# Row norms and loads reordered at the front, transposes ahead of values, and the last norms shared by three engines

## The chip, the cores and the metric
One core of a Trainium2 chip runs the whole program. The metric is the device time of one execution in microseconds (us), the median over runs.

## What is computed
One decoder block over 1024 tokens of width 1024, in float32, from `x`, 256 memory tokens `mem` and the weights. Cut to what matters:

```python
h = rms_norm(x, g_in);  proj = h @ w_in        # q,k,v of groups A,B,M, gate, index q,k,w
kvM = rms_norm(mem, g_mem) @ w_mem_kv
oA = dilated_mixture_attention(qA, kA, vA)     # 8 heads, three windows
oB = dsa_attention(qB, kB, vB, qI, kI, wI)     # 4 heads, top 256 keys by index score
oM = memory_attention(qM, kM, vM)              # 4 heads, 256 memory keys
o = concat(oA, oB, oM) * silu(gate)
return rms_norm(x + o @ w_out, g_final)
```

## The kernel before
The program is written by hand: each engine has its own instruction list, and semaphores join them. SyncE (SP) issues every DMA. Tokens are worked on in 8 tiles ("rows") of 128. Every large product is made three times, from a high and a low part of each operand (high x high, high x low, low x high), so each operand needs a high part (a copy on ScalarE, ACT) and a low part (a difference, on VectorE, DVE, or GpSimd, POOL).

**Front.** SP loads rows 0 to 3, weight tile 0, rows 4 to 7, the two memory rows, weight tile 1, two memory weights and, after a wait, weight tile 2 (L521 to L533). All weight tiles go through one buffer, `w_raw`; `load_w` (L504) waits until both parts of the tile before are made. `split_hi` (L736) makes the high part on ACT, `split_lo` (L643) the low part on POOL. The norm of a row is a sum of squares (`square_sum`: ACT L722 or DVE L992), a variance (DVE L971), a root (ACT L734), four small linked DVE instructions (L976 to L979) and a scaling of the row (DVE L1012); `scale_rows` does this for rows 0 and 1, 2 and 3, 4 to 7, and the memory rows. TensorE (PE) transposes the rows of a half (`turn`, L1307) into six PSUM banks; ACT makes the high part of each of the eight transposed blocks (`high`, L799), DVE the low part (`low`, L981). A bank comes free with its low part. `fill` (L1330) is a projection of one weight tile for one half of the tokens: fills 0 and 2 are tile 0 (halves 0 and 1), fills 1 and 3 tile 1. `evacuate` (L744) takes a fill out of PSUM, on ACT, and `split_low` (L1026) makes its low part, on DVE. `turn_mem` and `keep_mem` (L806) transpose the memory rows. The first index score needs the evacuation of w_i, which stands on ACT behind evacuation 3, the split of tile 3 and the eight `keep_mem`.

**Steps.** 8 pairs of heads (M, A, A, A, A, B, B, M) of 8 query tiles each are 64 steps; step 64 only finishes. On PE (loop at L1569) a step is: `scores` of step s, `turn_prob` (L1461) of the first four key tiles of step s-1, half of a fill, `values` (L1475) of these key tiles, then, if step s-1 had more than four key tiles, `turn_prob`, the other half of the fill and `values` for the rest. Not every step has a fill: those of pair 4 at tiles 4 and 5, pair 5 at 0 and 1, pair 6 at 2, 4, 6 and 7, and all of pair 7 have none. `values` waits for both copies of the transposed probabilities, head a by ACT (L899) and head b by DVE (L1198). DVE's step (loop at L1252) is: bias of head a (L1189 or L1176), copy, bias of head b, slots of the top-256 selection in pairs 0 to 5 (L1110 to L1144), second copy, the end of a group of four tiles (L1216, L1220), `split_low`. ACT's step is: copy, exponent of head a, second copy, exponent of head b, splits of weights, evacuation. In pair 6 the output weights are split too (ACT L939, low parts on POOL L706 and DVE L1289).

**End.** From step 56 on PE also does the output projection (`project_out`, L1527, 24 matmuls a unit), whose units DVE adds to the residual rows `y_rows` (`add_out`, L1222). In step 63 DVE norms rows 0 and 1 (`norm_rows`, L1246: variance, root on ACT, four links, final product L1243) and SP stores them. In step 64 come the last copy of probabilities and values, `turn_sums` (L1512), the end of the last group, POOL's `part_lo` (L668) and the last unit (3, 1). Then `project_last` (L1555) adds pair 7's part to rows 4 to 7, `add_last` (L1229) adds them, and rows 2 to 5 and 6 to 7 are normed in two chains. ACT squares each row (`square_row`, L877).

What orders the end on DVE and ACT are these lines:

```python
for n in range(len(LATE)):          # DVE L1297
    add_last(n)
norm_rows(1, 2, 6)
norm_rows(2, 6, 8)
```

## Time and profile before

| what | us |
|---|---|
| median of 3 runs | 780.11 (778.83 to 781.57) |
| profiled execution, its own time | 775.92 |
| span in the profile | 774.1 |
| busy: PE / DVE / ACT / POOL | 692.8 / 440.6 / 331.6 / 132.6 |
| mean granted TensorE clock | 0.969 |

The span runs from the first to the last instruction of one execution. Busy time is that of an engine's instructions without waits; matmuls overlap, so a busy PE is not PE at its peak. The granted clock is 1 at 2.4 GHz and 0.5 at 1.2 GHz.

### The profile page before, as it was taken

The page shows a single profiled execution, that of the slowest core. Times are in us where ns is not written, and L with a number is a line of the kernel's source. Part 1 is how long each engine was busy: PE and PEld are TensorE (multiplying, and loading weights), DVE is VectorE, ACT ScalarE, POOL GpSimd, SP SyncE. Part 2 cuts the span into 40 slices and gives each one's busy share as a digit, 9 for nine tenths or more (in the row PEclk, how much of TensorE's full clock was granted, in tenths as well). Part 3 has the DMA queues.
Part 4 walks back from the last instruction along what each step waited for, and adds up shares of the span by engine and source line. Part 5 has one row for each costly group of instructions (what it writes and reads, how often), then busy time and mean ns, then how long its engine had stood idle before and what let it go on. Part 6 is the DMA issues. An engine that isn't in the chain of part 4 may idle for free.

```text
span 774.1 us, 11520 instructions
## 1 busy us (share of the span) xinstructions
PE 692.8 (89%) x4261; PEld 546.9 (71%) x4261; DVE 440.6 (57%) x1003; ACT 331.6 (43%) x627; POOL 132.6 (17%) x90
## 2 busy tenths in 40 slices
PE   2879999999999999999999996979899868999972
PEld 2667788777777777777777774757677656777761
DVE  4856775265377448655876587679743354122237
ACT  4666565335335433543354353435444554121313
POOL 1121110111131122113111311031132124102000
PEclk9999999999999999999999997999999998999997
DMA  8311112111211022102212111010114206310014
GB/s 303 94 55 27 28 29 81 28 28 41 83 54 55 3 83 69 41 14 82 56 42 67 44 40 42 1 41 1 41 28 150 83 21 235 97 37 21 0 55 163
DMA packets 51863, 47.71 MB, mean 62 GB/s; under 512 B 5712, under 2 KB 44640, under 8 KB 51808
## 3 DMA queue, kind: packets, MB, share of 16 engines
q1 hardware_dynamic: 51808, 46.97, 19.4%
q8 instruction: 35, 0.57, 0.3%
q14 instruction: 20, 0.16, 0.1%
HBM read 39.62 MB, written 7.34 MB: 61 GB/s over the span
## 4 chain that ended last, share of the span: by engine, by line
PE 75%; DVE 12%; issue 5%; ACT 4%; DMA 1%; POOL 1%; DVEq 0%; SPq 0%; ACTq 0%; POOLq 0%
PE j_ps L1365 23%; PE s_ps L1365 8%; PE o_ps L1496 8%; PE pt_ps L1472 7%; PE s_ps L1401 5%; PE s_ps L1547 4%; PE j_ps L1547 4%; DVE picked L1114 4%; PE o_ps L1365 3%; PE s_ps L1420 3%; PE pt_ps L1420 2%; DVE probT L1198 1%; DVE prob L1189 1%; PE pt_ps L1518 1%; PE s_ps L1552 1%
## 5 line engine op out<-in xcount | busy, mean ns | idle before, releaser
L1365 PE MATMUL j_ps<-h_hi,w_hl 128*128 128x512 f32 (+2 forms) x640 | 210.4, 394 | 0.9 <-issue 0.9
L1365 PEld LDWEIGHTS j_ps<-h_hi,w_hl 128*128 128x128 f32 (+1 forms) x640 | 120.1, 189 | 25.5 <-issue 1.5
L647 POOL TENSOR_TENSOR w_hl<-w_raw,w_hl 128x1024 fp32r<-128x1024 f32 (+1 forms) x30 | 70.9, 2365 | 341.5 <-ACT w_hl L742 341.5
L1365 PE MATMUL j_ps<-h_lo,w_hl 128*128 128x512 f32 (+2 forms) x320 | 123.4, 386 | 0.0
L911 ACT ACTIVATE prob<-prob,nmax 128x256 f32<-128x256 f32 (+7 forms) x128 | 89.9, 703 | 50.9 <-DVE nmax L1189 47.3
L899 ACT ACTIVATE probT<-pt_ps 128x512 f32<-128x512 f32 (+3 forms) x88 | 41.4, 471 | 162.3 <-PE pt_ps L1472 161.8
L1472 PE MATMUL pt_ps<-ident,prob 128*128 128x128 f32 x496 | 75.8, 289 | 7.7 <-DVE gate L1216 7.3
L1365 PE MATMUL s_ps<-h_hi,w_hl 128*128 128x512 f32 x224 | 73.8, 398 | 0.4 <-POOL w_hl L647 0.4
L1472 PEld LDWEIGHTS pt_ps<-ident,prob 128*128 128x128 f32 x496 | 55.0, 144 | 24.8 <-issue 21.6
L1114 DVE TENSOR_SCALAR_CACHE_REDUCE picked<-idx,tk 128x384 f32<-128x384 f32 (+5 forms) x72 | 67.9, 943 | 1.6
L1365 PEld LDWEIGHTS j_ps<-h_lo,w_hl 128*128 128x128 f32 (+1 forms) x320 | 60.6, 189 | 11.1
L1198 DVE COPY probT<-pt_ps 128x512 f32<-128x512 f32 (+3 forms) x88 | 46.7, 531 | 27.5 <-PE pt_ps L1472 26.8
L1189 DVE CUSTOM_DVE_ANT_0 prob<-s_ps,bias 128x128 f32<-128x128 f32 (+7 forms) x64 | 47.1, 753 | 24.1 <-PE s_ps L1401 20.8
L1042 DVE SCALAR_TENSOR_TENSOR qk<-j_ps,qk 128x512 fp32r<-128x512 f32 (+2 forms) x28 | 17.7, 633 | 61.9 <-ACT qk L778 39.1
L1091 DVE SCALAR_TENSOR_TENSOR idx<-prob,w_i,idx 128x384 f32<-128x384 f32 (+5 forms) x42 | 40.2, 972 | 20.9 <-ACT prob L849 20.7
L1496 PE MATMUL o_ps<-probT,v_sb 128*64 128x128 f32 x576 | 42.8, 284 | 8.9 <-DVE probT L1198 7.8
L1496 PEld LDWEIGHTS o_ps<-probT,v_sb 128*64 128x64 f32 x576 | 31.1, 138 | 25.1 <-issue 22.7
L1365 PEld LDWEIGHTS s_ps<-h_hi,w_hl 128*128 128x128 f32 x224 | 42.1, 188 | 9.2 <-issue 0.6
L1365 PE MATMUL s_ps<-h_lo,w_hl 128*128 128x512 f32 x112 | 43.6, 390 | 0.0
L1496 PE MATMUL o_ps<-probT,v_b 128*64 128x128 f32 x288 | 22.6, 294 | 17.8 <-DVE probT L1198 17.8
L1401 PE MATMUL s_ps<-qk 64*128 64x512 f32 (+3 forms) x288 | 36.5, 376 | 0.0
L1365 PE MATMUL o_ps<-h_hi,w_hl 128*128 128x512 f32 (+1 forms) x96 | 33.8, 392 | 2.8 <-POOL w_hl L647 2.8
(233 smaller groups left out, 1091.7 us busy)
## 6 DMA issues: line engine op xcount, KB each, us to landing
w_raw<-in_w_in_dram SPq DMA_DIRECT2D x28, 512.0 KB, 3.9
idx<-in_x_dram SPq DMA_DIRECT2D x8, 512.0 KB, 5.9
bias<-in_a_tab_dram SPq DMA_DIRECT2D x8, 512.0 KB, 5.1
mixed_scratch<-gate SPq DMA_DIRECT2D x12, 256.0 KB, 2.2
bias<-in_x_dram SPq DMA_DIRECT2D x4, 512.0 KB, 8.3
probT<-in_w_mem_kv_dram SPq DMA_DIRECT2D x4, 512.0 KB, 6.3
bias<-in_w_out_dram SPq DMA_DIRECT2D x4, 512.0 KB, 3.8
out_dram<-idx SPq DMA_DIRECT2D x4, 512.0 KB, 2.8
```

The lines of the kernel that those rows point to most:

```text
L647: pool.tensor_tensor(w_hl[:, w % 2, 1, :, 0:n], w_raw[:, :, 0:n], w_hl[:, w % 2, 0, :, 0:n].bitcast(F32), ALU.subtract).then_inc(w_lo_read ...
L899: act.activation(probT[:, g % 2, 0, 0:n, :], pt_ps[0][:, 0:n, :], ACT.Copy).then_inc(pt_ready[0], 1)
L911: act.activation(prob[:, a, s % 2, 0:n], prob[:, a, s % 2, 0:n], ACT.Exp, scale=-1.0, bias=nmax[:, a, s % 2:s % 2 + 1], accum_out=lsum[:, ...
L1091: dve.scalar_tensor_tensor(out=x_slice(i), in0=relu[u % 4][:, 0:n], scalar=wt, in1=x_slice(i), op0=ALU.mult, op1=ALU.add).then_inc(idx_add ...
L1114: link(dve.tensor_scalar(some, xs, level, None, ALU.is_ge, ALU.add, accum_out=count))
L1189: dve.tensor_tensor_reduce(dst, s_ps[a][:, 0:n], table, scale, 3e38, ALU.add, ALU.min, low_out).then_inc(biased[a], 1)
L1198: dve.tensor_copy(probT[:, g % 2, 1, 0:n, :], pt_ps[1][:, 0:n, :]).then_inc(pt_ready[1], 1)
L1365: last = pe.matmul(bank[0:n, at:], a[:, k, 0:n], c[:, k, HALF * b + at:HALF * b + HALF], start=(k == 0 and q == 0), stop=(k == KD - 1 and ...
L1401: last[a] = pe.matmul(banks[a][:, keys], q[rows, tile], k[rows, keys], start=(m == 0), stop=(m == 2))
L1472: last = pe.transpose(pt_ps[a][:, n, :], prob[:, a, s % 2, P * k:P * k + P], ident[:, :])
L1496: last = pe.matmul(o_ps[DH * a:DH * a + DH, at], v, probT[:, g % 2, a, n, :], start=(k == 0), stop=(k == nk - 1))
L1547: pe.matmul(bank, a[:, p, :], wo_half(c, p, b), start=(p == 0 and q == 0), stop=False)
```

## The change
Three parts, in one diff.

1. Front: weight tile 1 gets a buffer of its own (`gate`, not yet in use) and is loaded right after tile 0, ahead of rows 4 to 7; tile 2 no longer waits for tile 1. Rows 0 to 3 share one norm chain. ACT scales the last row of each chain of four (rows 3 and 7), DVE the others. On ACT the split of tile 1 and the squares of rows 4 and 6 move ahead of the first eight high parts, the memory rows' root and evacuation 3 move forward. On DVE the square of row 5 moves ahead of the low parts. POOL waits for four scaled rows before its first split.
2. Steps: on PE the first `values` move behind the second `turn_prob` and the second half of the fill. This changes the order only where step s-1 had more than four key tiles.
3. End: rows 0, 1 and 2 are normed in step 64, behind the last copies of probabilities, with ACT's squares in step 63. Rows 3 to 7 share one chain; POOL multiplies rows 3 and 4 by the gain, ACT scales them, DVE does rows 5 to 7 as before.

```diff
-FINAL_ORDER = [0, 1, 2, 3, 4, 5, 6, 7]
+EARLY_ROWS = [0, 1, 2]
+SHARED_ROWS = [3, 4]
+LAST_ROWS = [5, 6, 7]
...
+        w_raws = [w_raw[:, :, :], gate[:, :].rearrange("p (k m) -> p k m", k=KD)]
...
+        def raw_of(w):
+            return w_raws[w == 1]
...
         def _(sp):
             def load_w(w):
-                if w:
-                    sp.wait_ge(w_hi_ready, w)
-                    sp.wait_ge(w_lo_ready, w)
+                if w >= 2:
+                    before = w if w > 2 else 1
+                    sp.wait_ge(w_hi_ready, before)
+                    sp.wait_ge(w_lo_ready, before)
                 at = 0
                 for c, n in W_TILES[w][2]:
-                    sp.dma_start(w_raw[:, :, at:at + n], w_k[:, :, c:c + n]).then_inc(w_in_sem, 16)
+                    sp.dma_start(raw_of(w)[:, :, at:at + n], w_k[:, :, c:c + n]) \
+                        .then_inc(w_second_in if w == 1 else w_in_sem, 16)
...
             load_w(0)
+            load_w(1)
             for r in range(NT // 2, NT + MT):
                 load_rows(r)
-            load_w(1)
+            load_w(2)
             load_wm(0)
             load_wm(1)
-            load_w(2)
...
-            for n, t in enumerate(FINAL_ORDER):
+            for n, t in enumerate(EARLY_ROWS):
                 sp.wait_ge(y_final, n + 1)
+                sp.dma_start(out_t[t], y_rows[t]).then_inc(stored, 16)
+            for n, t in enumerate(SHARED_ROWS):
+                sp.wait_ge(y_scaled, n + 1)
+                sp.dma_start(out_t[t], y_rows[t]).then_inc(stored, 16)
+            for n, t in enumerate(LAST_ROWS):
+                sp.wait_ge(y_final, len(EARLY_ROWS) + n + 1)
                 sp.dma_start(out_t[t], y_rows[t]).then_inc(stored, 16)
...
+            pool.wait_ge(x_ready, NT // 2)
             for w in range(PRE_W + 1):
                 split_lo(w)
...
             part_lo(STEPS)
+            for t in SHARED_ROWS:
+                pool.wait_ge(ysq_ready, t + 1)
+                pool.tensor_tensor(y_rows[t], y_rows[t], gf_row, ALU.mult).then_inc(y_gained, 1)
...
+            def scale_row(r, chain):
+                act.wait_ge(x_inverse, chain)
+                act.activation(x_raw[r], x_raw[r], ACT.Copy, scale=stat[:, 3, r:r + 1]).then_inc(x_ready, 1)
+
             square_sum(0)
             square_sum(2)
-            root(0, 2)
             square_sum(3)
+            root(0, 4)
             split_hi(0)
-            root(2, 4)
+            scale_row(3, 1)
+            split_hi(1)
+            square_sum(4)
+            square_sum(6)
             act.wait_ge(g_ready, 1)
             for v in range(KD):
                 high(v)
-            square_sum(4)
-            square_sum(6)
-            split_hi(1)
             root(4, 8)
             evacuate(0)
+            scale_row(7, 2)
             for v in range(KD, 2 * KD):
                 high(v)
             evacuate(1)
             square_sum(NT)
             square_sum(NT + 1)
+            root(NT, NT + MT)
             evacuate(2)
             split_hi(2)
-            root(NT, NT + MT)
+            evacuate(3)
             for k in range(KD):
                 keep_mem(k)
-            evacuate(3)
             split_hi(3)
...
+                if s == STEPS:
+                    y_root(0, 0, len(EARLY_ROWS))
                 if s in PART_AT:
                     part_hi(s)
                 if s == STEPS - 1:
-                    square_row(0)
-                    square_row(1)
-                    y_root(0, 0, 2)
+                    for t in EARLY_ROWS:
+                        square_row(t)
...
-            square_row(2)
-            for t in range(3, NT):
+            for t in range(len(EARLY_ROWS), NT):
                 square_row(t)
-                if t in (5, 7):
-                    y_root(1 + t // 7, 2 if t == 5 else 6, t + 1)
+            y_root(1, len(EARLY_ROWS), NT)
+            act.wait_ge(y_inverse, 1)
+            for n, t in enumerate(SHARED_ROWS):
+                act.wait_ge(y_gained, n + 1)
+                act.activation(y_rows[t], y_rows[t], ACT.Copy, scale=stat[:, 3, t:t + 1]).then_inc(y_scaled, 1)
...
                 inverse_root(a, b)
-                for r in range(a, b):
+                dve.drain().then_inc(x_inverse, 1)
+                for r in range(a, b if a >= NT else b - 1):
                     dve.tensor_scalar(x_raw[r], x_raw[r], stat[:, 3, r:r + 1], None, ALU.mult).then_inc(x_ready, 1)
...
-            scale_rows(0, 2, 1)
-            scale_rows(2, 4, 3)
+            scale_rows(0, 4, 3)
+            square_sum(5)
             for v in range(KD):
                 low(v)
-            square_sum(5)
             square_sum(7)
             scale_rows(4, 8, 5)
...
                 if early[1]:
                     add_out(*early[1])
+                if s == STEPS:
+                    start_norm(0, 0, len(EARLY_ROWS))
                 if s >= 1 and (s - 1) % 4 == 3:
                     finish_group(pair_of_step(s - 1)[0], (s - 1) % NT // 4)
+                if s == STEPS:
+                    dve.wait_ge(gf_in, 16)
+                    for t in EARLY_ROWS:
+                        final_norm(t)
                 if early[2]:
                     add_out(*early[2])
-                if s == STEPS - 1:
-                    norm_rows(0, 0, 2)
...
                 add_last(n)
-            norm_rows(1, 2, 6)
-            norm_rows(2, 6, 8)
+            start_norm(1, len(EARLY_ROWS), NT)
+            dve.drain().then_inc(y_inverse, 1)
+            for t in LAST_ROWS:
+                final_norm(t)
...
                     project_out(*early[0])
-                if s >= 1:
-                    values(s - 1, 0)
                 if two:
                     turn_prob(s - 1, 1)
-                if early[1]:
-                    project_out(*early[1])
                 if s < STEPS and projection_of_step(s):
                     if two:
                         fill(m, range(KD // 2, KD))
                     m += 1
+                if early[1]:
+                    project_out(*early[1])
+                if s >= 1:
+                    values(s - 1, 0)
                 if two:
                     values(s - 1, 1)
```

## Rows read from the trace of the kernel before

**Rows 1.** the page: busy time of the engines, and POOL's costliest group
```profile
PE 692.8 (89%) x4261; PEld 546.9 (71%) x4261; DVE 440.6 (57%) x1003; ACT 331.6 (43%) x627; POOL 132.6 (17%) x90
...
L647 POOL TENSOR_TENSOR w_hl<-w_raw,w_hl 128x1024 fp32r<-128x1024 f32 (+1 forms) x30 | 70.9, 2365 | 341.5 <-ACT w_hl L742 341.5
```

**Rows 2.** waits of PE: releaser, us in total, times, longest
```profile
PE o_ps L1496 <- DVE probT L1198: 29.9, 16, 4.4
```

**Rows 3.** timeline of the front: start us, us, engine, line, operation [idle before]
```profile
9.55 1.06 ACT L727 ACTIVATE prob<-idx 128x1024 f32<-128x1024 f32 x1 [0.17 <-DMA idx<-in_x_dram]
...
9.82 0.91 SPq L514 DMA_DIRECT2D bias<-in_x_dram  x2
...
12.17 0.99 DVE L977 SCALAR_TENSOR_TENSOR stat<-stat 128x2 f32<-128x2 f32 x1
...
13.59 1.42 DVE L1012 TENSOR_SCALAR idx<-idx,stat 128x1024 f32<-128x1024 f32 x2
...
16.28 1.48 ACT L803 ACTIVATE h_hi<-s_ps,g_cols 128x512 fp32r<-128x512 f32 x2 [4.34 <-PE s_ps L1314]
...
29.24 0.38 PE L1365 MATMUL o_ps<-h_hi,w_hl 128*128 128x256 f32 x1 [2.83 <-POOL w_hl L647]
...
33.71 0.27 PE L1314 MATMUL s_ps<-ident,picked 128*128 128x128 f32 x1
...
35.07 1.41 DVE L986 SCALAR_TENSOR_TENSOR h_lo<-s_ps,g_cols,h_hi 128x512 fp32r<-128x512 f32 x2 [0.56 <-ACT h_hi L803]
```

**Rows 4.** DMA issues of the first 30 us: count, size, us to landing
```profile
bias<-in_x_dram SPq DMA_DIRECT2D x2, 512.0 KB, 6.0
```

**Rows 5.** busy time by stretch: 10 to 19 us, with clock, DMA share, GB/s
```profile
10.00:19.00 9.00, 3.93 (x19) 3.94 (x20) 6.41 (x13) 3.87 (x8) 1.40 (x1) 1.00 1.01 369
```

**Rows 6.** timeline around the first index score
```profile
46.21 2.17 DVE L977 SCALAR_TENSOR_TENSOR stat<-stat 128x2 f32<-128x2 f32 x1
...
56.15 0.22 ACT L756 ACTIVATE w_i<-pt_ps 128x64 f32<-128x64 f32 x1
...
56.62 0.70 PE L1420 MATMUL s_ps<-kk_b,qk 128*128 128x384 f32 x2 [2.17 <-DVE qk L1042]
```

**Rows 7.** timeline, start of pair 5
```profile
502.78 1.39 DVE L1042 SCALAR_TENSOR_TENSOR qk<-j_ps,qk 64x512 fp32r<-64x512 f32 x2 [2.65 <-ACT qk L782]
...
506.43 3.26 POOL L694 TENSOR_SCALAR idx<-picked 128x896 f32<-128x896 f32 x1 [17.38 <-DVEq L1159]
...
512.47 1.76 DVE L1110 TENSOR_SCALAR rungs<-rungs,reach 128x13 f32<-128x13 f32 x1
```

**Rows 8.** timeline, end of pair 6
```profile
626.98 1.09 PE L1496 MATMUL o_ps<-probT,v_b 128*64 128x128 f32 x16 [1.78 <-DVE probT L1198]
...
629.26 0.66 PE L1496 MATMUL o_ps<-probT,v_b 128*64 128x128 f32 x8 [0.61 <-DVE probT L1198]
...
631.80 2.55 DVE L1289 SCALAR_TENSOR_TENSOR h_lo<-bias,h_hi 128x1024 fp32r<-128x1024 f32 x1 [2.69 <-ACT h_hi L939]
...
639.55 1.55 PE L1496 MATMUL o_ps<-probT,v_b 128*64 128x128 f32 x12 [0.74 <-DVE probT L1198]
...
648.73 1.09 PE L1496 MATMUL o_ps<-probT,v_b 128*64 128x128 f32 x16 [0.88 <-DVE probT L1198]
```

**Rows 9.** timeline of the end
```profile
746.03 0.77 PE L1496 MATMUL o_ps<-probT,v_m 128*64 128x128 f32 x8 [4.39 <-DVE probT L1198]
...
760.08 1.23 DVE L1234 TENSOR_TENSOR idx<-s_ps,idx 128x1024 f32<-128x1024 f32 x1 [0.16 <-PE s_ps L1566]
...
768.47 2.48 DVE L1243 SCALAR_TENSOR_TENSOR idx<-idx,stat,w_raw 128x1024 f32<-128x1024 f32 x2
```

**Rows 10.** DMA issues of the last 34 us: the stores of rows 4 to 7
```profile
out_dram<-idx SPq DMA_DIRECT2D x4, 512.0 KB, 2.8
```

**Rows 11.** busy time by stretch: the end, and one us of stores
```profile
742.00:764.00 22.00, 14.01 (x60) 10.84 (x60) 13.27 (x24) 7.99 (x16) 1.30 (x1) 0.91 0.12 49
...
771.00:772.00 1.00, 0.00 (x0) 0.00 (x0) 0.00 (x0) 0.00 (x0) 0.00 (x0) 0.50 1.00 401
```

More of the change, by code:

```diff
@@ L369, in build_program @@
         w_in_sem = sem("w_in_sem")
+        w_second_in = sem("w_second_in")
+        x_inverse = sem("x_inverse")
         w_hi_ready = sem("w_hi_ready")
@@ L417, in build_program @@
         y_final = sem("y_final")
+        y_gained = sem("y_gained")
+        y_inverse = sem("y_inverse")
+        y_scaled = sem("y_scaled")
         stored = sem("stored")
@@ L646, in split_lo @@
                 n = width(w)
-                pool.tensor_tensor(w_hl[:, w % 2, 1, :, 0:n], w_raw[:, :, 0:n],
+                pool.tensor_tensor(w_hl[:, w % 2, 1, :, 0:n], raw_of(w)[:, :, 0:n],
                                    w_hl[:, w % 2, 0, :, 0:n].bitcast(F32), ALU.subtract).then_inc(w_lo_ready, 1)
@@ L736, in split_hi @@
             def split_hi(w):
-                act.wait_ge(w_in_sem, 16 * sum(len(W_TILES[q][2]) for q in range(w + 1)))
+                if w == 1:
+                    act.wait_ge(w_second_in, 16)
+                else:
+                    act.wait_ge(w_in_sem, 16 * sum(len(W_TILES[q][2]) for q in range(w + 1) if q != 1))
                 if w >= 2:
@@ L741, in split_hi @@
                 n = width(w)
-                act.activation(w_hl[:, w % 2, 0, :, 0:n], w_raw[:, :, 0:n], ACT.Copy).then_inc(w_hi_ready, 1)
+                act.activation(w_hl[:, w % 2, 0, :, 0:n], raw_of(w)[:, :, 0:n], ACT.Copy).then_inc(w_hi_ready, 1)
             def evacuate(m):
@@ L1244, in final_norm @@
                                          op0=ALU.mult, op1=ALU.mult).then_inc(y_final, 1)
-            def norm_rows(n, a, b):
-                dve.wait_ge(gf_in, 16)
-                start_norm(n, a, b)
-                for t in range(a, b):
-                    final_norm(t)
             for s in range(STEPS + 1):
```

## The prediction

> **What bounds the kernel now.** I read the busy shares first: TensorE (PE) is busy for 692.8 of 774.1 us [rows 1], so time can only come out of its remaining 81 us. The waits of PE come second: its largest releaser is VectorE's (DVE's) copy of the transposed probabilities, 29.9 us in 16 waits, the longest 4.4 [rows 2]. The timelines then show where the idle time lies: a front up to the first index score at 56.62 [rows 3, 6], the steps of pairs 4 to 6 [rows 7, 8], and the end from 742 on [rows 9, 11]. Between these, in pairs 1 to 3 and from 650 to 742, matmuls follow one another, and a move of work between other engines is worth nothing there. The change touches all three places with idle time.
>
> **The front.** (a) One norm chain for rows 0 to 3 takes the place of two. The third square of ScalarE (ACT) starts at 9.55 and takes 1.06 plus 0.2 for its sum [rows 3]. Before, the second chain had a link of 0.99 us where its like take 0.16 [rows 3]: it ran into the first split product of GpSimd (POOL), which the new wait on four scaled rows keeps away. One chain is about 1.3 us, to 12.1; DVE scales three rows at 0.71 each (1.42 for two to 15.0 [rows 3]), ACT the fourth in 1.06 beside it: ready at 14.2, before at 15.0. Gain 0.8.
>
> (b) This gain is lost at once. The squares of rows 4 and 6 now stand ahead of the first half's eight high parts on ACT. Row 6 was issued at 9.82 [rows 3] and landed about 6.0 us later (median of rows 6 and 7) [rows 4], so near 15.5. The second weight tile, 512 KB at 369 GB/s [rows 5], comes in ahead of it and costs 1.4 to 1.8 us: row 6 is there at 17.1. The square ends at 18.35; the first high part, before at 16.28 [rows 3], starts 2.1 us late. On DVE the square of row 5 reads two SBUF operands, and POOL's two split products (1.4 us for the 72-column tile and 2.4 [rows 1]) run from 14.2 to 18.0. DVE operations of that kind are seen held to the end of a POOL product: 0.99 and 2.17 for 0.16 [rows 3, 6], 2.55 for 1.23 [rows 8]. I take the hold; the low parts then start at 19.7, not 17.0. The Trainium skill, SBUF — State Buffer, "Who interferes with whom", has the same pair as an exclusive lock for the whole instruction, won by whoever starts first. By that rule DVE could also win and hold POOL, and the sum would be 0.6 better.
>
> (c) What pays is the wait behind it. PE used to stand 2.83 us for the second tile's low part, and its next 24 matmuls took from 29.24 to 33.7 [rows 3], 0.19 us each, with a clock that had fallen in the wait. That tile is now split by 18.0. With eight low parts at 0.7 each (1.41 for two [rows 3]) from 19.7, the first fill ends at 26.9 (before 26.4), and the second follows without a wait, 24 matmuls at the full clock (0.12 each, an estimate), to 29.8. Rows 4 to 7: DVE is free of low parts at 25.3, square 1.65, chain 1.2, three scalings 2.1: 30.2, against a first transpose at 33.71 [rows 3]. Gain 3.5.
>
> (d) The memory rows' chain now stands ahead of ACT's evacuation and split. Its link of 2.17 under a POOL product [rows 6] goes, and with it PE's 1.9 us before their transposes. Evacuation 3 moves ahead of the eight keeps. The last thing before the first score stays ACT's evacuation of w_i: it ended at 56.37, the score started at 56.62 [rows 6]. New: fill 3 ends at 48.3 - 3.5 = 44.8, evacuation 1.2, eight keeps 3.0, split 1.06, w_i 0.2, which is 50.5, and the score at 50.8. **Front: -5.8.** Ends: -3.0 if the second tile costs twice as much of the load queue, -6.6 with no hold.
> The new wait of POOL has nothing behind it but these splits. SyncE's new place for tile 2 makes the memory weights wait until about 16, and nobody needs them before 100.
>
> **Transposes ahead of values.** No instruction is added. In steps with a fill the second values cost nothing either way. What changes there is that the fill ends one group of values (1.1 us) earlier, so that its evacuation and split do. In pairs 0 to 3 PE is without gaps, so nothing follows. In pair 4 the step without a fill waits for a DVE that is busy with the selection; a copy behind those slots is not earlier. Nothing.
> Pair 5: DVE idles 2.65 us for the evacuated query at 502.78 [rows 7]. With the fill 1.1 us earlier its split, bias and copy come 0.7 earlier (then the transposes bind), and so does POOL's mask at 506.43. The selection starts when POOL's split ends, at 514.2 (the 1.76 us row at 512.47) [rows 7], and PE follows this chain to 544. **-0.7**, ends 0 and -0.9. That PE's own wait before the second values at 508 shortens is worth nothing, since POOL's end starts the selection.
> Pair 6, steps 53 to 56, three of them without a fill. The waits before the second values, 0.61, 0.74 and 0.88 [rows 8], vanish, since the first values now cover the copy: 2.2. Beyond that, the earlier transposes release ACT's second exponent and then its output-weight splits by 0.9 us, and the DVE split that runs 2.55 us under a POOL product [rows 8] ends earlier by as much; the first wait (1.78 [rows 8]) shrinks by 0.7 by the earlier fill. Followed through to the end of the step at 650 I get 1.3 more. **-3.5**, ends -2.2 (the three waits alone) and -4.1.
>
> **The end.** Before, DVE normed rows 0 and 1 ahead of the last copy of probabilities, and PE stood 4.39 us until 746.03 [rows 9]. Now the copy goes first: values at about 742.5, -3.5. PE's clock was below full in this stretch, 0.91 over 22 us [rows 11], which is 2 us of work; most of that follows the stall, and I count 1.5. Against it: three final products of 1.24 [rows 9] stand ahead of the addition that opens rows 3 to 7, with POOL's 1.3 us product between them, which costs 0.5. So the last addition, at 760.08 [rows 9], comes at 755.6 and ends at 756.8. Square 1.25 to 758.1, chain 1.2 to 759.3.
> From there three last rows on DVE take 3.7 us, to 763.0, where before the last two began at 768.47 and ended at 770.95 [rows 9]. ACT scales rows 3 and 4 by 760.4 and 761.5, with POOL's two gain products (2.4 each, from 752.6) done by 757.5. But five stores now come together: one takes 2.7 to 2.8 us [rows 10] and each further one 1.3 (512 KB at 401 GB/s [rows 11]): 760.45 + 2.7 + 4 x 1.3 = 768.4. So the stores are late next, not DVE (763.0 + 2.8 = 765.8). The span ended at 774.1, 0.4 after the last landing: **-5.4**, ends -3.5 (the stall goes, and nothing else) and -6.7.
>
> **Sum.** 5.8 + 0.7 + 3.5 + 5.4 = 15.4 us. The profiled execution took 775.92, with a span of 774.1: 760.5 and a span near 758.7. It is 4.2 below the median of the runs, so the forecast for the median is 780.11 - 15.4 = 764.7. The ends add up to 8.7 and 18.3, or 771.4 and 761.8.
>
> **Rivals.** (1) DVE and ACT still set the pace in pairs 5 and 6 and the new order gives nothing: 15.4 - 4.2 = 11.2, 768.9. For it: the copies wait behind bias and weight splits on DVE. Against: three waits come after a DVE that idled. Chance 0.14. (2) The front is held by loads: row 6 lands at 20 instead of 17.1 because the strided weight tile goes through slowly, and ACT's high parts stand behind its square. Front -2.9, 767.6. For it: the queue is full throughout. Chance 0.13. (3) The end gives only its stall, 3.5 instead of 5.4, because POOL's products come late or hold DVE's chain: 766.6. Chance 0.12. (4) Slower: the same place as (2), one us of the whole for each us that row 6 is late. To eat 15.4 us it would have to land after 32, and nothing in the profile is that slow. That the whole lands within 0.3% would want 30. Chance 0.02, with 0.02 more for no change. The forecast as worked out has 0.57.
>
> 0.3% (2.3 us) is about what a measurement of this kernel can tell from no change. Faster by more 0.95, same 0.03, slower 0.02. The range reaches over (1) to (3) and over two of them together, and takes in the spread of the runs: 760.5 to 771.5.
>
> **What would show it.** First transpose near 14.2 and first high part near 18.3; no wait before the second fill; first index score near 50.8. The mask of pair 5 0.7 us closer to its step's start, and no waits before second values in pair 6. PE's wait of 4.4 us at the end below 1, the last final product near 763 and five stores back to back. The forecast is wrong if ACT waits for row 6 well past 17, if the score stays later than 53, or if the waits named as the probabilities' copies keep their 29.9 us.

## The result, and the profile after

The changed kernel takes 752.66 us, median of 4 runs (752.36 to 755.78); the kernel before, run beside it, 779.47 (4 runs, 778.33 to 781.57). The ratio is 0.9662, 95% interval [0.9628, 0.9696]: 26.8 us faster, where 15.4 were forecast. The forecast median was 764.7, and 760.5 was the low end of the range. The profiled execution of after took 752.36, with a span of 750.6. One run each of before, before_again and order_without_fill took between 1003 and 2340 us; the ratios leave these three slow runs out.

The page of after, its busy times; the span's 774.1 became 750.6 and PE's idle time went from 81 to 66 us:

```profile
PE 684.3 (91%) x4261; PEld 546.1 (73%) x4261; DVE 437.9 (58%) x989; ACT 335.5 (45%) x629; POOL 137.3 (18%) x92
```

PE's busy time fell too, by 8.5 us [rows 1], with the same 4261 matmuls. That is the first sign that idle time is not all that was saved: in the experiments below it changes with the granted clock and with the order of the same matmuls.

The waits of PE after (releaser, us in total, times, longest), which answer to [rows 2]:

```profile
PE o_ps L1532 <- DVE probT L1234: 13.1, 9, 3.7
PE s_ps L1350 <- DVE idx L1049: 11.8, 1, 11.8
PE pt_ps L1508 <- DVE gate L1252: 7.2, 9, 2.9
PE pt_ps L1508 <- DVE probT L1234: 5.5, 4, 3.0
```

The 29.9 us before the values are 13.1, and 5.5 of what went is back as a wait of the second transposes: their PSUM bank is free only when DVE has copied the first ones.

To compare kernels whose times shift, I read in each trace when PE starts the first index score, step 0, and the transposes of the sums that close each half of a pair, and took differences. Time of each stage in us, two profiles of each kernel (the second ones are the unchanged kernels run again, below); stages of a pair run from the close of the pair before to its own:

```
stage                        before  again    after  again   mean gain   forecast
start to first index score    56.62  57.91    51.00  52.03      5.8        5.8
index scores to step 0        89.75  86.66    86.61  88.21      0.8        0
step 0 to close of pair 3    291.44 290.79   287.73 287.47      3.5        0
pairs 4 and 5                147.34 147.62   146.23 144.93      1.9        0.7
pair 6                        64.59  67.75    60.53  59.76      6.0        3.5
pair 7 and the end           124.35 124.80   118.46 118.47      6.1        5.4
span                         774.10 775.54   750.57 750.87     24.1       15.4
```

**The front.** Timeline of after (columns as in [rows 3]):

```profile
12.65 2.08 DVE L1049 TENSOR_SCALAR idx<-idx,stat 128x1024 f32<-128x1024 f32 x3
14.79 3.42 PE L1350 MATMUL s_ps<-ident,idx 128*128 128x128 f32 x16 [11.75 <-DVE idx L1049]
...
16.18 2.36 POOL L668 TENSOR_TENSOR w_hl<-gate,w_hl 128x1024 fp32r<-128x1024 f32 x1
16.27 2.82 DVE L1031 CUSTOM_DVE_ANT_0 prob<-dist 128x512 f32<-128x512 f32 x1 [1.54 <-DMA dist<-in_x_dram]
17.54 1.06 ACT L752 ACTIVATE prob<-bias 128x1024 f32<-128x1024 f32 x1 [1.41 <-DMA bias<-in_x_dram]
...
18.59 2.41 ACT L831 ACTIVATE h_hi<-s_ps,g_cols 128x512 fp32r<-128x512 f32 x4
...
19.13 0.69 DVE L1033 CUSTOM_DVE_ANT_0 prob<-dist 128x512 f32<-128x512 f32 x1
...
20.06 2.73 DVE L1022 SCALAR_TENSOR_TENSOR h_lo<-s_ps,g_cols,h_hi 128x512 fp32r<-128x512 f32 x4
```

ACT's high parts wait for the square of row 6, which waits 1.41 us for its load. DVE's square of row 5 takes 2.82 us where its second half takes 0.69: it starts 0.09 us after POOL's product and ends at 19.09, 0.55 us after that one. Then the second fill follows the first without a wait, where [rows 3] had 2.83 us:

```profile
27.16 0.40 PE L1401 MATMUL j_ps<-h_hi,w_hl 128*72 128x512 f32 x1
...
27.39 0.28 PE L1401 MATMUL o_ps<-h_hi,w_hl 128*128 128x256 f32 x1
...
30.68 0.33 PE L1350 MATMUL s_ps<-ident,picked 128*128 128x128 f32 x1 [0.27 <-ACT bias L845]
...
51.00 0.59 PE L1456 MATMUL s_ps<-kk_b,qk 128*128 128x384 f32 x2 [1.64 <-ACT w_i L784]
```

**The end.** Timeline of after, which answers to [rows 9]:

```profile
724.76 0.66 PE L1532 MATMUL o_ps<-probT,v_m 128*64 128x128 f32 x8 [0.77 <-DVE probT L1234]
...
737.43 1.23 DVE L1270 TENSOR_TENSOR idx<-s_ps,idx 128x1024 f32<-128x1024 f32 x1
738.69 1.06 ACT L918 ACTIVATE qk<-idx 128x1024 fp32r<-128x1024 f32 x1 [0.21 <-DVE idx L1270]
...
741.25 3.67 DVE L1279 SCALAR_TENSOR_TENSOR idx<-idx,stat,w_raw 128x1024 f32<-128x1024 f32 x3 [0.16 <-DVE stat L1015]
...
742.36 0.33 SPq L650 DMA_DIRECT2D out_dram<-bias  x1
743.40 0.33 SPq L650 DMA_DIRECT2D out_dram<-idx  x1
743.78 2.74 SPq L653 DMA_DIRECT2D out_dram<-idx  x3
```

PE's wait of 4.39 is 0.77. DVE is done at 744.9, but the five stores, issued from 742.36 to 745.33, land at 745.02, 746.29, 747.59, 748.94 and 750.16, one every 1.3 us, and the span ends 0.4 later. In between the queue is full (busy time of one us; DMA share and GB/s are the last columns):

```profile
748.00:749.00 1.00, 0.00 (x0) 0.00 (x0) 0.00 (x0) 0.00 (x0) 0.00 (x0) 0.50 1.00 401
```

### The profile page after: what moved, and what is told of

Same layout as the page of the kernel before. It is cut to its first block, busy times and chain, and to the rows that moved or that the text cites. A ratio compares the mean times of both kernels' runs of the same rounds, so it can differ in the third digit from the quotient of the medians.

```text
span 750.6 us, 11512 instructions
## 1 busy us (share of the span) xinstructions
PE 684.3 (91%) x4261; PEld 546.1 (73%) x4261; DVE 437.9 (58%) x989; ACT 335.5 (45%) x629; POOL 137.3 (18%) x92
## 4 chain that ended last, share of the span: by engine, by line
PE 74%; DVE 12%; issue 5%; ACT 4%; POOL 2%; DMA 1%; SPq 1%; DVEq 0%; ACTq 0%; POOLq 0%
PE j_ps L1401 24%; PE s_ps L1401 8%; PE pt_ps L1508 7%; PE o_ps L1532 7%; PE s_ps L1437 5%; PE s_ps L1583 5%; PE j_ps L1583 4%; DVE picked L1150 4%; PE o_ps L1401 4%; PE s_ps L1456 3%; PE pt_ps L1456 2%; DVE prob L1225 1%; PE s_ps L1588 1%; DVE tk L1153 1%; PE pt_ps L1554 1%
## 5 line engine op out<-in xcount | busy, mean ns | idle before, releaser
L668 POOL TENSOR_TENSOR w_hl<-w_raw,w_hl 128x1024 fp32r<-128x1024 f32 (+1 forms) x29 | 68.2, 2353 | 327.3 <-ACT w_hl L770 314.8
L1401 PE MATMUL s_ps<-h_hi,w_hl 128*128 128x512 f32 x224 | 74.7, 402 | 0.3 <-POOL w_hl L668 0.3
L1225 DVE CUSTOM_DVE_ANT_0 prob<-s_ps,bias 128x128 f32<-128x128 f32 (+7 forms) x64 | 47.0, 753 | 26.8 <-PE s_ps L1437 23.9
L1234 DVE COPY probT<-pt_ps 128x512 f32<-128x512 f32 (+3 forms) x88 | 46.7, 531 | 14.8 <-PE pt_ps L1508 13.7
L1532 PE MATMUL o_ps<-probT,v_sb 128*64 128x128 f32 x576 | 40.1, 283 | 4.5 <-DVE probT L1234 4.5
L1401 PE MATMUL s_ps<-h_lo,w_hl 128*128 128x512 f32 x112 | 44.1, 394 | 0.0
L1583 PE MATMUL s_ps<-h_hi,w_hl 128*128 128x512 f32 x96 | 31.9, 400 | 0.0
```

Of the source, the lines that this page charges most:

```text
L668: pool.tensor_tensor(w_hl[:, w % 2, 1, :, 0:n], raw_of(w)[:, :, 0:n], w_hl[:, w % 2, 0, :, 0:n].bitcast(F32), ALU.subtract).then_inc(w_lo_ ...
L1225: dve.tensor_tensor_reduce(dst, s_ps[a][:, 0:n], table, scale, 3e38, ALU.add, ALU.min, low_out).then_inc(biased[a], 1)
L1234: dve.tensor_copy(probT[:, g % 2, 1, 0:n, :], pt_ps[1][:, 0:n, :]).then_inc(pt_ready[1], 1)
L1401: last = pe.matmul(bank[0:n, at:], a[:, k, 0:n], c[:, k, HALF * b + at:HALF * b + HALF], start=(k == 0 and q == 0), stop=(k == KD - 1 and ...
L1532: last = pe.matmul(o_ps[DH * a:DH * a + DH, at], v, probT[:, g % 2, a, n, :], start=(k == 0), stop=(k == nk - 1))
L1583: pe.matmul(bank, a[:, p, :], wo_half(c, p, b), start=(p == 0 and q == 0), stop=False)
```

## The experiments

Each kernel is timed against the kernel before, in runs on the same chip; the interval is the 95% one. A ratio can differ by up to 0.002 from the quotient of the medians. The question was where the 9 us by which the spans fell beyond the forecast (24.1 for 15.4) come from.

### The three parts alone, and the kernel before once more

Each is one part of the diff and nothing else: the row chains and loads (front_only), the order on PE (order_only), the last rows (end_only). before_again is the unchanged kernel.

> Only the order on PE is changed (values behind the second transposes and the second half of the fill); front and end are those of before. Theory: PE pays for each change between values and other matmuls, about 0.3 us in each of the 12 wide steps with a fill of pairs 1 to 3, so pairs 1 to 3 shorten by 3.7 us, pairs 4 and 5 by about 1.1 and pair 6 by about 4: -8.8 us, a span near 765.3. Rival (the prediction): steps with a fill are worth nothing, -4.2 us, a span near 769.9, and pairs 1 to 3 as long as before.

> Only the front of the change (loads, row chains, squares, memory chain). Theory: the first index score comes at 51.0 instead of 56.6 (-5.6), and pairs 1 to 3 stay as long as before. If the two falls of the clock in the index scores (from 56.9 and 77.4) stay away as in the changed kernel, 3.2 us more: -8.8 in all, a span near 765.3. Rival: the falls belong to the single execution and not to the change, then -5.6, a span near 768.5.

> Only the end of the change (rows 0 to 2 normed in step 64, one chain for rows 3 to 7, three engines). Theory: -5.9 us, of which PE's wait for the last copy of probabilities gives 3.6 and the fall of the clock behind it 1 to 1.5; everything up to 741 as before, a span near 768.2. Rival: the gain at the end needs the earlier parts (loads or clock), then -3.5.

> The kernel before, unchanged, with a profile of its own. Theory: the clock falls in the index scores come and go from one execution to the next, so this profile may lack one or both and be up to 3.4 us shorter up to 140 us; the profiled executions are no sure sign of the median. Rival: the falls come after the same waits every time, then the first 140 us agree with the first profile within 0.3 us. Ratio to before 1.000.

```
kernel        median  ratio    interval            span
order_only    766.78  0.9848   [0.9824, 0.9873]    764.8
front_only    773.83  0.9934   [0.9911, 0.9958]    770.6
end_only      771.45  0.9924   [0.9899, 0.9948]    769.7
before_again  778.54  1.0014   [0.9989, 1.0039]    775.5
```

The front alone gives 5.1 us (0.66% of 778.5) and the end 5.9: both near their terms, 5.8 and 5.4. The order alone gives 11.8, where its terms were 0.7 and 3.5. Multiplied, the three ratios make 0.9709, inside the interval of the second measurement of the whole (0.9703, below). So the error sits in the order on PE. order_only gives more than the 8.8 us that were expected of it, 11.8 in the medians and 9.3 in the spans.

before_again shows what a single profile is worth. Between the first index score and step 0 the kernel does the same in all of these (busy time of that stretch; after its length come PE, PEld, DVE, ACT, POOL, the granted clock, DMA share, GB/s). The kernel before:

```profile
56.60:146.40 89.80, 84.25 (x410) 72.06 (x410) 52.40 (x64) 48.00 (x71) 9.11 (x4) 0.96 0.13 36
```

before_again:

```profile
57.90:144.60 86.70, 81.16 (x410) 69.37 (x410) 52.36 (x64) 47.99 (x71) 9.11 (x4) 1.00 0.14 37
```

after:

```profile
51.00:137.60 86.60, 81.08 (x408) 69.31 (x409) 52.44 (x64) 47.99 (x71) 9.23 (x4) 1.00 0.14 37
```

order_only:

```profile
55.80:147.00 91.20, 85.69 (x408) 73.35 (x408) 52.00 (x64) 47.94 (x71) 9.05 (x4) 0.95 0.13 35
```

The idle time (length less PE) is 5.5 us in all four. What differs is PE's busy time, and with it the clock. In the traces the granted clock falls from 1 to 0.5 (1.2 GHz) for a short while. There are two such falls in the first row (at 56.95 and 77.43), none in the second and third, three in the fourth (55.58, 76.06 and 96.54). Each is worth about 1.5 us: 3.2 and 4.6 us of busy time above the rows that have none.

They are of two kinds. The later ones stand behind two waits of 1.8 us inside the stretch, which are the same in every kernel here. Behind these two, 5 of the 16 profiles of this document have no fall, 7 have one and 4 have two, with the old front (5 falls in 7 profiles) and with the new (10 in 9). Nothing ties those to the change. The first one belongs to the front: each of the seven profiles with the old front has a fall that starts between 51.1 and 57.0, behind the memory rows' chain and the wait for w_i, in some before the first index score and in some behind it. Of the nine with the new front only memory_old_place (below), which puts that chain back, has one there, at 48.34. So of the 3.1 us by which after beats the first profile of before in this stretch, half is that fall and half is chance.

### Which steps gain from the order

Two kernels have the new order in one kind of step each: in steps with a fill, or in those without (`late = not (...)`).

```diff
-                if s >= 1:
+                late = bool(s < STEPS and projection_of_step(s))
+                if s >= 1 and not late:
                     values(s - 1, 0)
                 if two:
                     turn_prob(s - 1, 1)
-                if early[1]:
-                    project_out(*early[1])
...
+                if early[1]:
+                    project_out(*early[1])
+                if s >= 1 and late:
+                    values(s - 1, 0)
```

A third, values_between, puts the first values between the second transposes and the second half of the fill. The transposes come early, as in the change, but PE still goes to the values twice.

```diff
-                if s >= 1:
-                    values(s - 1, 0)
                 if two:
                     turn_prob(s - 1, 1)
-                if early[1]:
-                    project_out(*early[1])
+                if s >= 1:
+                    values(s - 1, 0)
...
+                if early[1]:
+                    project_out(*early[1])
```

> The new order on PE only in steps that have a fill; without a fill, front and end as before. Theory (each visit to the values costs PE a change of kind): the second halves of pairs 1 to 3 take 41.6 instead of 42.8 us each, so -3.7 there and about -1.5 in pairs 4 and 5; pair 6 changes only by its earlier fill, -0.7. Together -5.5 to -6. Rival (the prediction's step): 0 in pairs 1 to 3.

> The new order on PE only in steps without a fill (2 in pairs 4 and 5, 3 in pair 6). Theory: the second halves of pairs 1 to 3 stay at 42.8; the three waits before second values in pair 6 go, and with them falls of the clock, so pair 6's second half (37.8 and 41.1 us in the two profiles of before) takes 34 to 35.5: -3 to -6 us in all. Rival: without the earlier fill the first waits in pair 6 grow by what the others lose, then -1 to -2 only.

> Second transposes ahead of the first values as in the change, but both groups of values kept apart by the second half of the fill; front and end as before. Theory: the gain of pairs 1 to 3 comes from having one visit to the values per step and not from earlier transposes, so most of it goes: second halves of 42.5 to 42.9 us. Pair 6's steps without a fill have the new order, so -3 to -6 us there. Rival: earlier transposes bring it, then 41.6.

```
                     median  ratio   interval          2nd half of pairs 1, 2, 3   2nd half of pair 6
before (2 profiles)    -       -                       42.81 to 42.85              37.83, 41.13
order_with_fill      772.61  0.9907  [0.9875, 0.9939]  41.58 to 41.60              39.68
order_without_fill   773.07  0.9922  [0.9893, 0.9950]  42.80 to 42.85              34.89
values_between       773.44  0.9926  [0.9898, 0.9954]  43.03 to 43.05              35.31
after (2 profiles)     -       -                       41.58 to 41.63              33.76, 32.96
```

Pairs 1 to 3 gain 1.2 us each in exactly the half that has more than four key tiles, only where steps with a fill have the new order, and nothing (they even lose 0.2) where the transposes are early but the values stay apart. PE is without gaps there in both kernels (0.29 and 0.28 us idle in the second half of pair 1), and the granted clock is 1.00 in both. So neither a wait nor the clock is behind it; it is the second visit to the values. Timeline of PE in one such step (pair 1, six key tiles), the kernel before:

```profile
261.03 0.39 PE L1365 MATMUL j_ps<-h_hi,w_hl 128*128 128x512 f32 x1
261.35 1.09 PE L1496 MATMUL o_ps<-probT,v_sb 128*64 128x128 f32 x16
262.38 0.66 PE L1472 MATMUL pt_ps<-ident,prob 128*128 128x128 f32 x4
262.79 0.48 PE L1365 MATMUL j_ps<-h_hi,w_hl 128*128 128x512 f32 x1
...
265.40 0.39 PE L1365 MATMUL j_ps<-h_hi,w_hl 128*128 128x512 f32 x1
265.72 0.66 PE L1496 MATMUL o_ps<-probT,v_sb 128*64 128x128 f32 x8
266.31 0.66 PE L1509 MATMUL pt_ps<-ident,vT 128*128 128x128 f32 x4
```

The same step after:

```profile
251.97 0.40 PE L1401 MATMUL j_ps<-h_hi,w_hl 128*128 128x512 f32 x1
252.20 0.60 PE L1508 MATMUL pt_ps<-ident,prob 128*128 128x128 f32 x4
252.56 0.47 PE L1401 MATMUL j_ps<-h_hi,w_hl 128*128 128x512 f32 x1
...
255.18 0.39 PE L1401 MATMUL j_ps<-h_hi,w_hl 128*128 128x512 f32 x1
255.50 1.53 PE L1532 MATMUL o_ps<-probT,v_sb 128*64 128x128 f32 x24
256.96 0.66 PE L1545 MATMUL pt_ps<-ident,vT 128*128 128x128 f32 x4
```

Read the starts, not the durations. From the last matmul of a fill to the next instruction is 0.32 us if that is a value (261.03 to 261.35), and 0.23 if it is a transpose (251.97 to 252.20). From the first transpose to the fill behind it are 0.41 us before and 0.36 after. The value groups take 1.03 and 0.59 us before, 1.62 in all; the one group after takes 1.46. Added up: 0.09 + 0.05 + 0.16 = 0.30 us for one visit fewer, and 12 such steps (four in each of pairs 1 to 3) make 3.6 us, where the two pairs of profiles have 3.7 and 3.3. From one matmul of a fill to the next is 0.22 to 0.23 us (timeline of before), so a transpose comes no later behind a fill than another fill matmul would, and a value does.

The three kernels were expected to give 5.5 to 6, 3 to 6 and 3 to 6 us; their ratios give 7.2, 6.1 and 5.8. The first two multiply to 0.9830, where order_only has 0.9848.

Pair 6 gains most where steps without a fill have the new order, as forecast. Its second half, by stretch (columns as above), in the kernel before:

```profile
611.90:649.80 37.90, 28.39 (x229) 21.94 (x227) 20.23 (x32) 19.59 (x34) 12.51 (x6) 0.89 0.19 59
```

before_again:

```profile
609.60:650.70 41.10, 31.49 (x228) 24.10 (x226) 20.31 (x32) 19.53 (x34) 12.93 (x6) 0.81 0.21 72
```

after:

```profile
598.30:632.10 33.80, 27.90 (x228) 21.90 (x227) 20.13 (x32) 19.08 (x34) 11.66 (x5) 0.90 0.17 54
```

after_again:

```profile
599.40:632.40 33.00, 26.90 (x228) 21.11 (x226) 20.05 (x32) 18.88 (x34) 11.67 (x5) 0.93 0.17 55
```

PE's idle time is 9.5 and 9.6 before, 5.9 and 6.1 after: 3.6 and 3.5 us less. Its busy time, with the same matmuls, is 28.4 and 31.5 before, 27.9 and 26.9 after. The profile that I forecast from was a lucky one here: a clock of 0.89 where the same kernel had 0.81 the next time. On the mean of these pairs 2.5 us of busy time went with the waits, where the clock is higher. More profiles bear it out on the mean, though not one by one: the four with the old order in all steps are busy for 28.3 to 31.5 us here (mean 30.3), the nine with the new order for 26.9 to 29.5 (mean 28.0).

The waits that remain are of the kind that [rows 2] did not have (timeline of after):

```profile
621.40 0.52 PE L1508 MATMUL pt_ps<-ident,prob 128*128 128x128 f32 x3 [2.96 <-DVE probT L1234]
621.85 3.18 PE L1532 MATMUL o_ps<-probT,v_b 128*64 128x128 f32 x28
...
629.58 0.63 PE L1508 MATMUL pt_ps<-ident,prob 128*128 128x128 f32 x4 [1.87 <-DVE probT L1234]
```

### What the front owes to what

From here on the kernels are the changed one with a single edit. memory_old_place puts the memory rows' root and evacuation 3 back:

```diff
-            root(NT, NT + MT)
             evacuate(2)
             split_hi(2)
-            evacuate(3)
+            root(NT, NT + MT)
             for k in range(KD):
                 keep_mem(k)
+            evacuate(3)
```

tile_behind_rows loads tile 1 behind the rows again and splits it behind the high parts, still in a buffer of its own:

```diff
             load_w(0)
-            load_w(1)
             for r in range(NT // 2, NT + MT):
                 load_rows(r)
+            load_w(1)
...
-            split_hi(1)
             square_sum(4)
...
             for v in range(KD):
                 high(v)
+            split_hi(1)
```

squares_behind moves ACT's square of row 6 behind the eight high parts, and DVE's square of row 5 behind the low parts.

> The changed kernel with the memory rows' root and evacuation 3 back in their old places on ACT. Theory: the four links of the memory chain meet POOL's split product again and ACT's evacuation 3 stands behind the keeps, so the first index score comes at 53.5 to 54.5 instead of 51.0, the rest unchanged: +3 us. Rival: PE's transposes of the memory rows are hidden anyway, 0.

> The changed kernel with weight tile 1 loaded behind all rows (still in its own buffer) and its split on ACT behind the first high parts. Theory: row 6 lands 1.3 us earlier, the first high part starts near 17.3 instead of 18.6, the tile's low part is ready near 26.5, when the first fill ends: first index score within 0.7 us of 51.0 either way. Rival (the prediction's step c): the early tile is what pays in the front, then the wait of 2.8 us before the second fill and a fall of the clock return, and the score comes 3 us later.

> The changed kernel with ACT's square of row 6 and DVE's square of row 5 behind the first half's high and low parts. Theory: the first high part starts near 16.3 instead of 18.6 and PE's 1.9 us wait before the first fill goes, but DVE's work up to the scaled rows 4 to 7 stays the same and binds: first transpose of the second half near 29.5 instead of 30.7, first index score near 50.0, -1 us. Rival: the squares were in nobody's way, 0.

```
kernel            median  ratio   interval           span   first index score
memory_old_place  757.71  0.9738  [0.9713, 0.9762]   753.8  53.29
tile_behind_rows  754.88  0.9694  [0.9670, 0.9717]   753.4  51.90
squares_behind    751.80  0.9668  [0.9638, 0.9699]   749.7  49.33
```

The first score moves from one execution to the next: five profiles with the changed front as it stands (front_only among them) have it at 50.20 to 52.03, seven with the old front at 55.82 to 57.91. Much of that is there before these edits act, as PE's first transpose comes at 13.9 to 14.8 in the five. So I read from that transpose to the first score. That takes 36.2 to 36.5 us in four of the five, and 37.8 in after_again, where the clock fell at 20.59.

The memory rows' and evacuation's place is worth 2.7 us (39.0), with the fall of the clock at 48.34 in it; its first score at 53.29 is just short of the 53.5 to 54.5 expected. The early load of tile 1 is worth about 0.7 (37.05), in one profile; 3 were expected. Without it POOL splits the tile from 24.63 to 27.32, and PE waits 0.49 us for it where it waited 2.83 before. So most of that wait did not go by the early load: ACT makes the tile's high part at 23.50 there, right behind the eight high parts, and at 25.31 before, where the squares of rows 4 and 6 stood in between. The squares ahead of the high parts cost 1.0 (35.27 here and 35.35 in two_chains_squares, below, which has its first score at 49.63). With them behind, the square of row 6 waits for nothing, the high parts start at 16.11 instead of 18.59, and DVE's square takes its plain time, now outside POOL's products (timeline of squares_behind):

```profile
15.05 1.06 ACT L752 ACTIVATE prob<-picked 128x1024 f32<-128x1024 f32 x1 [0.67 <-DMA picked<-in_x_dram]
...
16.11 2.40 ACT L831 ACTIVATE h_hi<-s_ps,g_cols 128x512 fp32r<-128x512 f32 x4
...
22.22 0.68 DVE L1031 CUSTOM_DVE_ANT_0 prob<-dist 128x512 f32<-128x512 f32 x1
```

That part of the change is a loss inside a gain. But the 1.0 us don't stand out in the whole: 0.9668 against 0.9662 and, measured again, 0.9703.

### What the end owes to sharing

five_on_vector leaves all five last rows to DVE, with POOL's and ACT's share taken out. two_chains norms rows 3 and 4 in a chain of their own, ahead of the last two additions; DVE does row 3, and row 4 stays shared. two_chains_squares has the squares of squares_behind as well.

```diff
-            start_norm(1, len(EARLY_ROWS), NT)
-            dve.drain().then_inc(y_inverse, 1)
-            for t in LAST_ROWS:
+            start_norm(1, len(EARLY_ROWS), NT)
+            for t in SHARED_ROWS + LAST_ROWS:
                 final_norm(t)
```

```diff
             for n in range(len(LATE)):
                 add_last(n)
+                if n == 1:
+                    start_norm(1, len(EARLY_ROWS), LAST_ROWS[0])
+                    dve.drain().then_inc(y_inverse, 1)
-            start_norm(1, len(EARLY_ROWS), NT)
-            dve.drain().then_inc(y_inverse, 1)
+            final_norm(SHARED_ROWS[0])
+            start_norm(2, LAST_ROWS[0], NT)
```

> The changed kernel with all five last rows normed by VectorE, POOL and ACT doing none. Theory: the five stores set the end, and VectorE makes a row every 1.24 us while a store takes 1.3, so the span is within 0.5 us of the changed kernel's. Rival: sharing the norms saves two products, so +2.5 us without it.

> The changed kernel with rows 3 and 4 normed in a chain of their own between the late additions (row 3 on VectorE, row 4 by POOL and ACT), rows 5 to 7 in a second chain. Theory: five stores in a row set the end now, so two of them earlier let the last three end 1.5 to 2 us sooner: 23.2 to 23.7 us from the start of the last group's sums to the end instead of 25.2. Rival: the extra chain delays the late additions by as much as it brings, 0 or worse.

> The version the experiments point to: two chains at the end, and the squares of rows 5 and 6 behind the high and low parts at the front. Theory: -1.7 and -1.0 us against the changed kernel, a median near 750.0, ratio to before near 0.964. Rival: one of the two brings nothing, 751 to 752.

> The changed kernel unchanged, with a second profile. Theory: its profile free of clock falls between 50 and 138 us was luck; this one shows 86.6 us from the first index score to step 0 plus 1.5 to 1.7 for each fall (0 to 2 of them), with the waits at the same places; all stages without a fall agree within 0.1 us. The median stays near 752.7, the ratio near 0.967. Rival: the new front keeps the clock up in the index scores, then 86.6 again.

```
kernel              median  ratio   interval           close of pair 7 to the end
five_on_vector      753.81  0.9686  [0.9662, 0.9711]   25.28
two_chains          754.04  0.9698  [0.9655, 0.9742]   25.88
two_chains_squares  753.72  0.9689  [0.9645, 0.9732]   25.88
after_again         753.75  0.9703  [0.9654, 0.9752]   25.22
```

Sharing the last rows by three engines is worth nothing: 25.28 against 25.21. DVE alone takes 1.2 us a row and the queue 1.3, so with DVE alone the stores still land back to back, from 746.48 to 751.62. What the end gained came with the rest of that part, as end_only has 25.22 too, where the two profiles of before have 27.4 and 27.5.

Two chains lose 0.67, where a gain of 1.5 to 2 was expected, and two_chains_squares misses its expected 750.0 as well. The extra chain runs into POOL's gain product (timeline of two_chains, DVE):

```profile
735.51 0.17 DVE L1016 RECIPROCAL stat<-stat 128x2 f32<-128x2 f32 x1 [0.27 <-ACT stat L924]
735.71 1.81 DVE L1017 SCALAR_TENSOR_TENSOR stat<-stat 128x2 f32<-128x2 f32 x1
737.56 0.16 DVE L1018 SCALAR_TENSOR_TENSOR stat<-stat 128x2 f32<-128x2 f32 x1
```

POOL, beside it:

```profile
735.12 2.39 POOL L740 TENSOR_TENSOR idx<-idx,w_raw 128x1024 f32<-128x1024 f32 x1 [5.38 <-ACT qk L920]
```

A link of 0.16 us takes 1.81, to POOL's end at 737.51. No version is clearly better than the changed kernel. after_again has one fall of the clock in the index scores and 88.21 us there, as expected.

## Why the prediction was wrong

**(a) to (d), the front: right in the main, 5.6 and 5.9 for 5.8.** The high parts start at 18.59 (forecast 18.35), the low parts at 20.06 (19.7), the first fill ends at 27.4 (26.9), the second follows without a wait, the next transposes at 30.68 (30.2), the first score at 51.00 (50.8). The hold on the square of row 5 was assumed from three rows, and is there: 2.82 for 0.69. By the rule of the Trainium skill, SBUF — State Buffer, "Who interferes with whom", whoever starts first wins; POOL started 0.09 us earlier and won, so the rule and the trace agree, and its other outcome (0.6 better) is not what was seen. Two sums are slightly off: 9.82 + 6.0 is 15.8 and not 15.5 in (b), which with the tile gives 17.2 to 17.6 (the square started at 17.54), and (d) adds up to 50.3 and not 50.5. Left out was the fall of the clock behind the memory rows' chain, which goes with it. In the working of (c) one credit was misplaced: I gave the vanished wait to the tile "now split by 18.0", and tile_behind_rows keeps all but 0.7 us with a split that ends at 27.3.

**Order of values, steps with a fill: the step that failed.** It read: "In steps with a fill the second values cost nothing either way", and "In pairs 0 to 3 PE is without gaps, so nothing follows." Both came from counting waits. Without gaps does not mean without cost: a value starts 0.32 us behind a fill's last matmul where the fill's own follow each other at 0.22 or 0.23, and two groups of values take 0.16 us more than one of the same 24. The runs show 3.5 us there on the mean, the most that any term was off. order_with_fill has it, order_without_fill and values_between don't.

**Pairs 4 and 5: the mechanism right, the size short.** The selection of pair 5 starts at 514.2 - 467.69 = 46.5 us behind the middle of pair 4 before, and at 500.65 - 454.92 = 45.7 after (500.65 is again the end of POOL's split, 498.28 + 2.37): 0.8 closer, forecast 0.7. And as forecast, the shorter waits of PE before the values there are worth nothing by themselves: 2.2 us go in pair 4 and 1.15 come back in the first half of pair 5, which waits for the selection. The rest of the 1.9 lies in pair 5's second half and in one of its two profiles, 44.1 us where the other has 45.6. No run isolates it, and some of it is chance: before has 45.6 and 45.7 there, but end_only, with the old order, has 44.7.

**Pair 6: mechanism right, mis-sized.** The idle time fell by 3.6 and 3.5, forecast 3.5. What the sum left out is the clock, which was lower where those waits stood: 3.5 became 4.1 against the one profile and 6.0 against the mean of two.

**The end: right.** 5.9 and 6.3 us for 5.4. The stall is 0.77, the stores end it: 742.36 + 2.66 + 4 x 1.3 = 750.2, measured 750.16. That the stores would be late next is why the help of ACT and POOL is worth nothing, as five_on_vector shows; the forecast had not drawn that.

**The reference.** The sum ran against one profiled execution that stood 4.2 us below its median, and I took its stages for those of any execution. But pair 6 took 3.2 us less in it than in the second profile, and the index stretch 3.1 more: the spans nearly agree, the stages don't. Against the mean of two profiles the terms were short by 3.5 (steps with a fill), 2.5 (pair 6), 1.2 (pairs 4 and 5), 0.8 (index stretch) and 0.7 (end): 8.7, the distance from 15.4 to 24.1. The 0.8 is the fall at 56.95, half of 1.5 as only one of the two profiles of before has it behind the first score; the chance falls cancel, one in each pair. Against the forecast median of 764.7 the miss is 12.0. The other 3.3 us are a difference between medians and profiles in the first measurement (780.11 - 752.66 = 27.45 against 24.1); in the second the medians differ by 23.8.

The rivals: (1), that the order gives nothing, is refuted (0.9848 for it alone). (2) is not what happened, though row 6 does hold ACT for 1.41 us. (3) is refuted (0.9924). (4) needed row 6 after 32; it was there at 17.5.

**What stays open.** Why one more visit to the values costs PE 0.3 us: shown is where, how often and how much. A value matmul has weights of 128*64, those of fills and transposes are 128*128, but no run changes the one without the other. And the 3.7 us between the product of the parts (0.9709) and the first measurement of the whole (0.9662), most of which is gone in the second (0.9703).

## What to carry to other kernels

On a busy PE count visits, not only waits: the same matmuls in fewer groups of a kind are faster, here by 0.3 us per visit. Where waits go, look whether the clock was low around them. A second profile of the unchanged kernel shows how much of a stage is luck, before anything is forecast from it. When three engines share a task at the end of a kernel, first divide its bytes by the rate of the store queue: if that sets the end, one engine may do.

## What the hardware showed that was not expected

- From a fill's last matmul to a value's first 0.32 us, to a transpose's 0.23; two value groups of 16 and 8 take 1.62 us where one of 24 takes 1.46.
- Behind the same two waits of 1.8 us TensorE's clock fell never, once or twice, in 5, 7 and 4 of 16 profiles, about 1.5 us each.
- DVE work of 0.16 to 0.69 us took 1.81 and 2.82 beside a POOL product and ended 0.01 and 0.55 us after it; moved out of it, the square took 0.68.
